# PSUM operands for VectorE's one-hot comparisons, index passes and prompt dot products in a two-layer diffusion step with expert retrieval

## The reference, cut to what matters

```python
def one_block(xb):                      # 128 tokens
    q = (xb @ w_pq).reshape(TOK_BLOCK, PEER_HEADS, 2, D_KEY_HALF)
    s = jnp.einsum('thcd,hcnd->thcn', q, sub_keys).astype(jnp.float32)
    s1, i1 = lax.top_k(s[:, :, 0], PEER_TOPK)
    s2, i2 = lax.top_k(s[:, :, 1], PEER_TOPK)
    cand_s = (s1[..., :, None] + s2[..., None, :]).reshape(TOK_BLOCK, PEER_HEADS, PEER_TOPK * PEER_TOPK)
    cand_i = (i1[..., :, None] * N_KEYS + i2[..., None, :]).reshape(TOK_BLOCK, PEER_HEADS, PEER_TOPK * PEER_TOPK)
    top_s, pos = lax.top_k(cand_s, PEER_TOPK)
    eidx = jnp.take_along_axis(cand_i, pos, axis=-1)
    g = jax.nn.softmax(top_s, axis=-1)
    u = jnp.take(u_exp, eidx, axis=0)
    a = jax.nn.gelu(jnp.einsum('thkd,td->thk', u, xb).astype(jnp.float32))
    w = (g * a).astype(xb.dtype)
    return jnp.einsum('thk,thkd->td', w, jnp.take(v_exp, eidx, axis=0))
```

## Time and profile before

| | us |
|---|---|
| median of 3 runs | 4217.21 |
| lowest and highest | 4215.59, 4217.39 |
| profiled execution | 4209.3 |
| its span, first to last instruction | 4207.5 |
| mean granted TensorE clock | 0.987 |
| TensorE busy / VectorE / ScalarE / GpSimd | 4015.6 / 2789.8 / 1751.2 / 2321.4 |

### The profile page before, as it was taken

One profiled execution on the slowest core, in us unless ns is written; L12 is line 12 of the kernel. 1 busy time (PEld: TensorE's weight loads), 2 busy tenths in 40 slices (PEclk: granted clock), 3 DMA queues, 4 the chain that ended last, 5 costly groups with the idle time before them and its releaser, 6 DMA issues.

```text
span 4207.5 us, 57280 instructions
## 1 busy us (share of the span) xinstructions
PE 4015.6 (95%) x21230; PEld 3364.7 (80%) x21230; DVE 2789.8 (66%) x4311; ACT 1751.2 (42%) x3014; POOL 2321.4 (55%) x1112
## 2 busy tenths in 40 slices
PE   7978999999999899999989999999999989999997
PEld 5757898888888788877769989888888878887875
DVE  3773239889898566566643322989989867676665
ACT  3264324756657322322231132374655732222223
POOL 1101225676767666666643322576676767666664
PEclk9999999999999999999999999999999999999999
DMA  5303235867768988888844312486776898888884
GB/s 207 113 1 126 86 101 165 280 224 244 261 222 284 315 280 288 277 282 286 297 145 180 102 59 88 146 294 216 256 251 226 277 321 275 284 286 276 289 295 157
DMA packets 385364, 921.99 MB, mean 219 GB/s; under 512 B 29296, under 2 KB 161136, under 8 KB 370800
## 3 DMA queue, kind: packets, MB, share of 16 engines
q1 hardware_dynamic: 310432, 647.48, 46.0%
q0 software_dynamic: 73728, 268.47, 18.8%
q10 hardware_dynamic: 976, 3.15, 0.2%
HBM read 776.64 MB, written 142.34 MB: 218 GB/s over the span
## 4 chain that ended last, share of the span: by engine, by line
PE 32%; issue 30%; POOL 29%; DVE 4%; DMA 3%; ACT 1%; DVEq 0%; POOLq 0%; ACTq 0%
PE PS L736 21%; POOL SL L427 17%; POOL ROWS L434 9%; PE PS L544 5%; PE PS L728 4%; POOL SL L418 3%; DMA ROWS<-u_exp,EI 2%; PE PS L748 2%; DMA ROWS<-v_exp,EI 1%; PE PS L695 1%; DVE OH L1196 1%; DVE ROWS L1205 1%; DVE EQ L1177 0%; DVE EQ L1173 0%; ACT SH L963 0%
## 5 line engine op out<-in xcount | busy, mean ns | idle before, releaser
L427 POOL TENSOR_TENSOR SL<-RW,SH 128x1024 fp32r<-128x1024 f32 x512 | 1409.3, 2753 | 922.7 <-ACT SH L963 901.1
L963 ACT CAST SH<-RW 128x1024 fp32r<-128x1024 f32 x512 | 537.4, 1050 | 1063.8 <-PE PS L736 537.7
L736 PE MATMUL PS<-HH,SH 128*128 128x512 f32 x2048 | 815.9, 398 | 28.3 <-POOL SL L427 28.2
L748 PE MATMUL PS<-WH,SH 128*128 128x512 f32 x2048 | 811.2, 396 | 11.0 <-DVE WL L1255 5.6
L748 PE MATMUL PS<-WL,SH 128*128 128x512 f32 x2048 | 809.4, 395 | 0.0
L748 PE MATMUL PS<-WH,SL 128*128 128x512 f32 x2048 | 809.4, 395 | 0.0
L736 PE MATMUL PS<-HL,SH 128*128 128x512 f32 x2048 | 801.5, 391 | 0.0
L736 PE MATMUL PS<-HH,SL 128*128 128x512 f32 x2048 | 801.4, 391 | 0.0
L1211 DVE SCALAR_TENSOR_TENSOR ACC<-ROWS,AA,ACC 128x1024 f32<-128x1024 f32 x256 | 369.7, 1444 | 528.8 <-DMA ROWS<-v_exp,EI 522.3
L418 POOL TENSOR_TENSOR SL<-RW,SH 128x1024 fp32r<-128x1024 f32 x84 | 202.6, 2416 | 816.5 <-ACT SH L788 816.5
L1196 DVE TENSOR_TENSOR OH<-CO,PK 128x1024 f32<-128x1024 f32 x256 | 575.7, 2290 | 96.1 <-PE PS L728 88.0
(11 more groups left out here) (161 smaller groups left out, 5203.4 us busy)
## 6 DMA issues: line engine op xcount, KB each, us to landing
RW<-u_blk SPq DMA_DIRECT2D x256, 512.0 KB
RW<-v_blk SPq DMA_DIRECT2D x256, 512.0 KB
gate_acts<-GE SPq DMA_DIRECT2D x256, 256.0 KB
router_weights<-GT SPq DMA_DIRECT2D x64, 1024.0 KB, 5.2
GB<-router_weights SPq DMA_DIRECT2D x32, 2048.0 KB, 12.3
GL<-gate_acts SPq DMA_DIRECT2D x256, 256.0 KB
RW<-wstream SPq DMA_DIRECT2D x100, 512.0 KB
AW<-wpairs SPq DMA_DIRECT2D x40, 1024.0 KB, 5.1
```

Source lines behind the costliest of these rows:

```text
L427: nc.gpsimd.tensor_tensor(SL[:, r % 2], RW[:, r % RAW], SH[:, r % 2].bitcast(F32), ALU.subtract).then_inc(raw_used, 1)
L736: last = mm(PS[:, n % 2], w[:, n % 2, j], a[:, j, 0:NS], start=(j == 0 and q == 0), stop=(j == DJ - 1 and q == 2))
L748: last = mm(PS[:, dj], w[:, k % 2, dj], a[:, k], start=start, stop=stop)
L963: nc.scalar.copy(SH[:, r % 2], RW[:, r % RAW]).then_inc(hi_done, 1)
```

## The change

Four operands of VectorE move from SBUF to PSUM, the other operand of each instruction stays in SBUF:

- the prompt tokens: `HTOK_PS` is PSUM banks 2 and 3, where the transposes leave them. ScalarE's copy to `HTOK` and the semaphore `ht_done` are gone.
- `IOTA_PS`, the numbers 0 to 127, in bank 4, written once a layer by TensorE (identity times `IOTA`) behind the transposes, after a wait for the last score copy that used the bank. `J16` is its first 16 columns.
- `IF`, the indices as fp32, in bank 4 beside it, written by VectorE's cast.

The transposed picks go to bank 5 instead of bank 2. VectorE's wait for the prompt tokens (now `ht_ps`) stands ahead of the first routing pass, where it stood ahead of the first one-hots. The line numbers of the kernel after are one to three higher from here on.

```diff
-    IF, _ = sb("IF", [P, HC, TOPK], F32)
...
-    J16 = IOTA[:, 0:TOPK]
+    HTOK_PS = PSf[:, 1024:2048]
+    IOTA_PS = PSf[:, 2048:2048 + NKEY]
+    J16 = IOTA_PS[:, 0:TOPK]
+    IF = PSf[:, 2176:2176 + HC * TOPK].rearrange("p (i k) -> p i k", k=TOPK)
...
             for j in range(DJ):
                 last = nc.tensor.transpose(PSf[:, 1024 + j * P:1024 + (j + 1) * P], H[:, j, NS:NT], ID)
+            pe.wait_ge(sc_done, 2 + l * HC + N_PQ - 1)
+            last = mm(IOTA_PS, ID, IOTA, start=True, stop=True)
             last.then_inc(ht_ps, 1)
...
                 pe.wait_ge(pick_ready, l * 4 + t + 1)
-                pe.wait_ge(ht_done, l + 1)
...
-                    last = nc.tensor.transpose(PSf[:, 1024 + q * P:1024 + (q + 1) * P], src, ID)
+                    last = nc.tensor.transpose(PSf[:, 2560 + q * P:2560 + (q + 1) * P], src, ID)
...
-            act.wait_ge(ht_ps, l + 1)
-            nc.scalar.copy(HTOK[:], PSf[:, 1024:2048]).then_inc(ht_done, 1)
...
-            v.tensor_copy(IF[:], I16[:])
+            v.tensor_copy(IF, I16[:])
...
-                v.tensor_tensor(OH[:, par], IOTA.unsqueeze(1).unsqueeze(1).to_broadcast(shape),
+                v.tensor_tensor(OH[:, par], IOTA_PS.unsqueeze(1).unsqueeze(1).to_broadcast(shape),
...
-                v.tensor_tensor_reduce(ROWS[:, n % RING], ROWS[:, n % RING], HTOK[:], 1.0, 0.0, ALU.mult, ALU.add,
+                v.tensor_tensor_reduce(ROWS[:, n % RING], ROWS[:, n % RING], HTOK_PS, 1.0, 0.0, ALU.mult, ALU.add,
...
+            dve.wait_ge(ht_ps, l + 1)
             route_slot(0)
             route_slot(1)
-            dve.wait_ge(ht_done, l + 1)
```

More of the change, by code:

```diff
@@ L230, in hybrid_step @@
     x_saved, x_back = sem("x_saved"), sem("x_back")
-    ht_ps, ht_done = sem("ht_ps"), sem("ht_done")
+    ht_ps = sem("ht_ps")
     sm_in, sm_out = sem("sm_in"), sem("sm_out")
@@ L994, in picks_out @@
                 act.wait_ge(pick_ps, l * 4 + t + 1)
-                nc.scalar.copy(PK[:, t % 2].rearrange("p q t -> p (q t)"), PSf[:, 1024:1024 + 3 * P]).then_inc(pick_done, 1)
+                nc.scalar.copy(PK[:, t % 2].rearrange("p q t -> p (q t)"), PSf[:, 2560:2560 + 3 * P]).then_inc(pick_done, 1)
             def w_high(n):
@@ L1170, in route @@
             dve.drain()
-            fi = IF[:].rearrange("p (h c) k -> p h c k", c=2)
+            fi = IF.rearrange("p (h c) k -> p h c k", c=2)
             for c in range(2):
```

## The result

| | before | after |
|---|---|---|
| median of 4 runs each, run beside each other, us | 4217.3 (4215.59 to 4221.63) | 4191.21 (4190.6 to 4193.04) |
| ratio, 95% interval | | 0.9937 (0.992 to 0.9955) |
| profiled execution, its span, us | 4209.3, 4207.5 | 4190.61, 4188.8 |

The kernel after is 26.1 us faster, and the interval of the ratio reaches from 19 to 34 us; the forecast was 17 (4200, with a range of 4191 to 4211, at whose edge this lies). Run again beside nine runs of before it gave 0.9939 (0.9925 to 0.9952). So the direction held, and so did the rank of the causes that had been priced, and the size was too small by a third.

A forecast was written before the change was run, and what follows sets the result against it. TensorE's matmul pace was taken to bound the kernel. Terms of -8.6 us in layer 0 and -8.1 in layer 1, together about -17, took the median from 4217.2 to 4200 us, range 4191 to 4211.

The forecast's parts named there:

- the clock behind the gap: TensorE's slow granted clock after the idle time ahead of block 0: counted 0, bounds -2 and 0 us a layer.
- the candidate sum: L1153 in the routing passes keeps two SBUF operands and its loss, 0.1 to 0.55 us each.
- The mechanism: Two-SBUF-operand VectorE instructions and GpSimd's subtraction never run together, the second waits; one PSUM operand parts them.
- a PSUM operand doesn't part the engines: Rival: the change doesn't do what it says, only the copy goes, -2 us, 4215 us; chance 0.08.
- half rate: Rival: VectorE reads PSUM at half rate in these forms, 128 gate blocks lose 0.96 each, about 4338 us; chance 0.04.
- Start: Ahead of block 0: without ScalarE's copy of the prompt tokens the first split starts earlier, -1.0 us a layer.
- Routing passes: Blocks 7 to 20: GpSimd's stretched subtraction no longer ends after TensorE wants it, -1.2 and -0.7 us.
- First gathers: Block 21's gate matmuls no longer wait, as indices and rows come about 4 us earlier: -1.1 us a layer.
- Gate blocks from 48 on: First gate block of the other three segments: one-hots no longer wait for GpSimd, -3.1 us a layer.
- Tail: The last 20 gathered rows, up to v's start: shorter ring rounds, partly lost to full DMAs, -2.2 us a layer, bounds 0 and -5.
- the one that gave the whole tail and the clock's dip: Rival: the tail gives all and the slow clock at the start goes, -25.5 us, 4192 us; chance 0.12.
- the fourth rival: Gains are there but new collisions with GpSimd's subtraction and later landings take their place: -7 us, 4210 us; chance 0.10.

The follow-up runs named there:

- e0: The kernel before again, no edit, for a second profile: 4217.19 us, ratio 1.0004 to before.
- e5: The kernel after with ScalarE's copy of the prompt tokens put back ahead of the first split, read by nobody: 4199.97 us, ratio 0.9955 to before.
- e7: The kernel after with a ring of five row buffers instead of four: 4193.67 us, ratio 0.9941 to before.
- e4: The kernel after again, no edit, as mate of the runs beside it: 4189.95 us, ratio 0.9939 to before.
- e6: The kernel after with two gathered rows in each gate block instead of three to every two: 4168.28 us, ratio 0.9881 to before.
- e9: The kernel after with SyncE's first read-back of gates and activations moved from block 122 to the last u block: 4199.48 us, ratio 0.9967 to before.
- e10: e6 with ScalarE's first split put ahead of the last two score copies: 4156.43 us, ratio 0.9867 to before.
- e1: The kernel before with only the prompt tokens in PSUM, their copy gone and the picks in bank 5: 4205.72 us, ratio 0.9976.
- e11: The kernel before with ScalarE's copy of the prompt tokens moved behind the second split, operands still in SBUF: 4212.31 us, ratio 0.9995.

## Why the prediction was right in its mechanism, and where it was wrong

Over the two u stages and the gaps ahead of them the first profiles differ by 61.9 - 38.4 = 23.5 us; the prediction's terms came to 16.7. Two steps failed most: the clock behind the gap was counted as 0 and measured -2.6 us, and the candidate sum was said to keep its loss, of which 2.45 us went.

- *The mechanism* held, in both orders of start. All 256 one-hots and all 256 row products are at 1.22 us, all 20 L1174 and all 20 L1178 at 2.29; 255 of 256 gathers of the u stage are at 0.95 us (before, 132 had 1.8 and 12 had 2.8), and 248 of 256 subtractions there at 2.4. The rivals "a PSUM operand doesn't part the engines" and "half rate" fell with these rows: at half rate L1206 would show some 2.4 us.
- *The price of a PSUM operand*, taken as nothing, is nothing: 1220 and 1218 ns with one, against 1.21 to 1.23 us for the same one-hots and row products of before where nothing met them. The 65 ns that the Trainium skill ("VectorE: DVE Perf Modes", TRN2 errata) would add do not show. The index cast went from 0.30 to 0.43 us, as bounded.
- *Start*: -1.0 a layer forecast, -1.2 measured. *Routing passes*: -1.2 and -0.7 forecast, -1.35 and -1.45 measured. *First gathers*: -1.1 each forecast, -1.6 and -1.35 in blocks 20 to 47. *Gate blocks from 48 on*: -3.1 each forecast, -3.6 and -3.8 measured. In the last three 2.9 us together lie beyond the forecast, and 2.45 of them (0.8 and 1.65) are at the blocks where L1153 had met a subtraction. The text had "the candidate sum L1153, keeps two SBUF operands and its loss". It kept the operands but hardly any loss, since the sums had moved by 0.8 to 1.3 us against TensorE's blocks. That such a loss hangs on the place in the block e0 shows from the other side: there three sums of the unchanged kernel had moved by 2.9 us and cost nothing, and losses at other blocks took their place. It can come back, too: e5 loses 0.3 us more at blocks 39 and 40 of layer 0 and 0.1 in layer 1, e7 0.3 at blocks 95 and 96. **A residual collision was carried over as if its place in the block were fixed.**
- *The clock behind the gap*: "I count 0 (bounds -2 and 0 a layer)". Measured -1.1 and -1.6, 2.6 us together, and much the same in e4. This is the largest mis-sized term. The row to read it from stood in the trace of before: block 0 alone took 8.0 us in layer 0 at a granted clock of 0.68. **An effect with a one-sided bound was taken at its end instead of inside.** Why the shorter gap spared it stays open: in e6 and e7, with the same gap, block 0 lost about what it lost in before, in layer 0 more, and there the 0 would have been right.
- *Tail*: -2.2 each, measured -1.8 and -3.6, 1.0 us more together. With e0 and e4 in place of the first profiles it is 4.0 instead of 5.4, so this term is right within the scatter. The forecast's reading was half right. It said that the ring's pace sets the start of v and that full DMA engines take half of the gain back. e7 and e9 show that ring and read-back bound it jointly, which fits a tail that gets no more than this from shorter gathers; no run shortened the gathers of the tail alone.
- *The baseline*: "The profiled execution was 4209.3 in all, 7.9 below the median of the runs; I carry the difference over." e0's profile shows that 3.9 us more of collisions in blocks 20 to 120 stand in a run that is nearer to the median, and the kernel after has none of them in either of its profiles. **The 7.9 us were treated as untouched by the change.** Of the 8.8 us between 4200 and 4191.2, 6.9 are the terms above; the remaining 1.9 fit in this, which is not shown, and they are far inside the interval of the medians' difference (19 to 34 us).
- *The rivals*: nearest in time was the one that gave the whole tail and the clock's dip, 4192. Its second half nearly came true (2.6 us of its 3), its first didn't: the tail gave 5.4 us, where that rival had 9.9 (4.4 in the forecast and 5.5 more; the prediction's own ring rounds, 4.3 and 5.2, make 9.5). The new collisions of the fourth rival exist (two of the ten candidate sums now wait, 3.4 and 3.6 us for 2.28) and cost TensorE nothing.

So in the first profiles every term, taken over both layers, was too small: start 0.4, clock 2.6, routing passes 0.9, first gathers 0.75, gate blocks 1.2, tail 1.0. They were added up from the blocks of one profile, and that one stood at the low end of before's runs.

## What to carry to other kernels

Where GpSimd works beside VectorE, look for two-operand VectorE instructions whose mean is well above their shortest, and put one operand of each in PSUM if a bank is free; it cost nothing here, and the gain is the few places where the wait breaks a chain that the bounding engine needs, plus room for moving work. That room was worth nearly as much as the change itself: 21 to 22 us for one number in a table, beside the change's 26. Before you trust a sum of stalls, profile the kernel before twice and ask of every difference between the profiles whether the change would remove it.

## What was not expected of the hardware

**A gather's issue waits too.** In the trace of before, a gather that GpSimd issued beside a row product with two SBUF operands took 1.76 us for 0.95; with the operand in PSUM 0.95 beside the same work. The tensor_tensors hold it as well. This gather was issued beside the first one-hot of the earlier trace rows, which ended near 904.0:

```profile
903.05 1.76 POOL L434 DMA_INDIRECT ROWS<-u_exp,EI  x1
```

Of the 157 gathers of before's u stages that took more than 1.5 us, 120 ended 0.81 to 0.83 us behind a one-hot comparison, 25 behind a row product and 12 behind an index pass. The Trainium skill ("SBUF — State Buffer", section "Who interferes with whom") infers that a tensor_tensor leaves descriptor generation alone. The trace of before differs, for the tensor_tensors and for the custom row product, and the measurement decides.

**Block 0 and the granted clock.** Below are the matmuls of block 0 in both layers: of before (idle 4.5 us ahead of it), of the kernel after (3.3), of e6 (3.3) and of e10 (0.0).

```profile
603.33:611.32 7.99, 7.99 (x24) 6.39 (x25) 0.68 0.46 131
2615.11:2622.26 7.15, 7.15 (x25) 5.75 (x25) 0.76 0.50 148
```

```profile
604.43:611.37 6.94, 6.93 (x25) 5.61 (x25) 0.79 0.54 151
2608.89:2614.46 5.57, 5.57 (x24) 4.62 (x25) 1.00 0.63 188
```

```profile
603.79:612.28 8.49, 8.49 (x25) 6.70 (x25) 0.63 0.42 124
2596.95:2603.95 7.00, 7.00 (x25) 5.69 (x25) 0.78 0.52 151
```

```profile
598.18:603.72 5.54, 5.54 (x25) 4.60 (x25) 1.00 0.20 44
2585.12:2590.68 5.56, 5.56 (x25) 4.60 (x26) 1.00 0.17 49
```

Without idle time block 0 runs at 2.4 GHz throughout. Behind 4.5 us it spends a part at 1.2 GHz in every profile. Behind 3.3 us the kernel after, e1, e4, e9 and e11 lose 1.5 and 0.1 us, e6 and e7 2.9 to 3.0 and 1.6, although the instructions up to block 0 of layer 0 are the same in after and e6. What decides it isn't settled by these runs. So in five of the seven profiles with the short gap the 1.2 us of copy were worth more than 1.2 us, and in e6's and e7's they weren't; the last 3.3 us of idle time were worth 5.5 a layer (e10 against e6).

**Four small loads can hold a queue for 20 us.** The four loads of 256 KB in e7 kept SyncE's queue for 20.18 us, behind a 2 MB load of gates, beside gathers and at a DMA share near 1 (1.03 to 1.10 between 1382 and 1406), and what stood behind them was the chunk that TensorE needed.
